# Block 1 attention: the reciprocal row sums are widened on GpSimd and turned by two more half transposes in the next unit's run, in place of two spreading matmuls

## What is computed

```python
s = jnp.einsum('bqhgd,bkhd->bhgqk', qi, k_all)
p = softmax_f32(s, v_all.dtype)
return jnp.einsum('bhgqk,bkhd->bqhgd', p, v_all)
```

## Time and profile before

| | |
|---|---|
| median of 3 runs | 2471.14 us |
| lowest, highest | 2470.4, 2471.89 us |
| profiled execution, its time | 2470.0 us |
| its span, first to last instruction | 2468.2 us |
| TensorE matmul, weight load | 2403.5, 1965.8 us busy |
| VectorE, ScalarE, GpSimd | 1337.6, 948.7, 470.7 us busy |
| mean granted TensorE clock | 0.992 |

### The profile page before, as it was taken

How to read it: one execution, slowest core, us unless ns; L and a number is a source line. 1 busy time by engine, 2 the same in 40 slices (tenths; PEclk the granted TensorE clock), 3 DMA queues, 4 the chain that set the end, 5 groups by cost and what they waited for, 6 DMA issues and landing times.

```text
span 2468.2 us, 39988 instructions
## 1 busy us (share of the span) xinstructions
PE 2403.5 (97%) x16150; PEld 1965.8 (80%) x16150; DVE 1337.6 (54%) x2653; ACT 948.7 (38%) x1659; POOL 470.7 (19%) x287
## 2 busy tenths in 40 slices
PE   8999999999999999999999999999999999999998
PEld 6778878888877788888887678888888667888887
DVE  5677667655236655667549444333336844433333
ACT  5473272632233724463453334222225323322222
POOL 2101211012342022103563231000014241000001
PEclk9999999999999999999999999999999999999999
DMA  8303413043233053306332112233232112223222
GB/s 316 113 2 124 167 50 120 22 159 140 64 116 137 2 205 112 117 35 239 105 139 81 52 60 88 90 96 104 89 99 96 60 52 69 94 77 120 94 79 75
DMA packets 64648, 250.49 MB, mean 101 GB/s; under 512 B 7888, under 2 KB 10448, under 8 KB 54992
## 3 DMA queue, kind: packets, MB, share of 16 engines
q1 hardware_dynamic: 61216, 236.10, 27.4%
q0 software_dynamic: 2592, 11.54, 1.4%
q10 hardware_dynamic: 656, 0.30, 0.1%
HBM read 243.67 MB, written 4.19 MB: 100 GB/s over the span
## 4 chain that ended last, share of the span: by engine, by line
PE 86%; ACT 4%; DVE 3%; issue 3%; POOL 2%; DMA 1%; ACTq 0%; SPq 0%; DVEq 0%; POOLq 0%
PE ps L2656 38%; PE ps L2467 21%; PE ps L593 5%; PE ps L692 4%; PE ps L2633 4%; PE ps L634 3%; ACT probs L866 2%; PE ps L677 2%; PE ps L2446 1%; PE ps L2349 1%; POOL split_panels_first L1121 1%; DMA stage_low<-in_ada 1%; PE ps L2673 1%; PE ps L2488 1%; PE ps L2601 1%
## 5 line engine op out<-in xcount | busy, mean ns | idle before, releaser
L2656 PE MATMUL ps<-h_split,split_panels 128*128 128x512 f32 x2928 | 685.6, 393 | 1.7 <-ACT projected L1580 0.7
L2656 PEld LDWEIGHTS ps<-h_split,split_panels 128*128 128x128 f32 x2928 | 545.9, 188 | 126.6 <-issue 13.6
L2467 PE MATMUL ps<-h_split_first,split_panels_first 128*128 128x512 f32 (+1 forms) x2772 | 543.6, 353 | 3.8 <-POOL h_split_first L1153 2.0
L2467 PEld LDWEIGHTS ps<-h_split_first,split_panels_first 128*128 128x128 f32 x2772 | 443.8, 189 | 78.1 <-issue 9.5
L1121 POOL TENSOR_TENSOR split_panels_first<-panels_first,split_panels_first 128x1024 fp32r<-128x1024 f32 (+1 forms) x102 | 229.0, 2246 | 711.7 <-ACT split_panels_first L1308 711.7
L1990 DVE TENSOR_TENSOR split_panels<-panels,split_panels 128x1024 fp32r<-128x1024 f32 (+2 forms) x171 | 192.6, 1126 | 297.0 <-ACT split_panels L1316 293.3
L1316 ACT ACTIVATE split_panels<-panels 128x1024 fp32r<-128x1024 f32 (+2 forms) x210 | 204.2, 974 | 344.9 <-PE ps L2656 343.5
L1814 DVE SCALAR_TENSOR_TENSOR ps<-modulation_panels,silu_c,ps 128x256 f32<-128x256 f32 x480 | 225.3, 488 | 29.7 <-issue 1.3
L2656 PE MATMUL ps<-ffn_hidden_split,split_panels 128*128 128x512 f32 x990 | 225.0, 389 | 0.0
L2656 PEld LDWEIGHTS ps<-ffn_hidden_split,split_panels 128*128 128x128 f32 x990 | 185.8, 188 | 38.6
L1132 POOL TENSOR_TENSOR probs_turned<-probs_turned,probs 128x512 f32<-128x512 f32 x30 | 42.3, 1411 | 771.3 <-ACT probs L1523 771.3
(11 more groups left out here) (304 smaller groups left out, 2975.2 us busy)
## 6 DMA issues: line engine op xcount, KB each, us to landing
modulation_panels<-in_ada SPq DMA_DIRECT2D x64, 1024.0 KB, 4.8
panels<-in_w SPq DMA_DIRECT2D x88, 512.0 KB, 3.3
panels_first<-in_in SPq DMA_DIRECT2D x72, 512.0 KB, 5.7
panels<-in_in SPq DMA_DIRECT2D x42, 512.0 KB, 3.3
panels_first<-in_out SPq DMA_DIRECT2D x32, 384.0 KB, 3.1
panels<-in_w SPq DMA_DIRECT2D x32, 384.0 KB, 3.1
panels<-in_w SPq DMA_DIRECT2D x32, 320.0 KB, 2.8
panels<-in_out SPq DMA_DIRECT2D x16, 512.0 KB, 3.3
```

The lines of the kernel that those rows point to most:

```text
L2467: ins = mm(at0, split1[:, s, w, c, :], hs1[:, h, c, lo:e], start=c == 0 and i == 0, stop=c == KC - 1 and i == 2)
L2656: ins = mm(out, split[:, n % SPLIT, a, c - base, :], moving(b, c), start=first and i == 0 and j == 0, stop=last and i == len(chunks) - 1 a ...
```

## The change

GpSimd gets one more task per unit. It multiplies ones by the column of reciprocals, repeated 64 times, for each head, and writes both into `wide_weights` (128x128). It waits for `weight_ready` and, since there is one buffer, until the run that read its last content has ended. TensorE's run for `prev` now starts with a half transpose of `wide_weights` partitions 0 to 63 of `old` into the output bank and ends with that of partitions 64 to 127; the pairs between are shifted by one. Before the run TensorE waits for the values, for `y_done`, for `weights_wide` and for `exp_done`, and before its last half for `low_weights`, which its own first half raises. `outputs_pe` makes no spreading matmuls for block 1. The last unit of a mixer gets a run of this one pair. Block 2 keeps its spreading.

```diff
-        def turn_halves_pe(pe, u):
-            pe.wait_ge(exp_done, 2 * u["u"] + 2)
+        def turn_halves_pe(pe, u, old):
             low, high, n_third = [], [], 0
+            if old:
+                pe.wait_ge(values_taken, old["values_seen"])
+                if old["i"] >= 1:
+                    pe.wait_ge(y_done, old["u"])
+                pe.wait_ge(weights_wide, old["u"] + 1)
+                low.append((bank(old["out_bank"], P, P + HD), wide_weights[0:HD, :]))
+            if u:
+                pe.wait_ge(exp_done, 2 * u["u"] + 2)
...
+            if old:
+                high.append((bank(old["out_bank"], P + HD, 2 * P), wide_weights[HD:P, :]))
             for n, two in enumerate(zip(low, high)):
...
+                for half, (to, src) in enumerate(two):
+                    if old and half == 1 and n == len(high) - 1:
+                        pe.wait_ge(low_weights, old["u"] + 1)
+                    ins.append(nc.tensor.transpose(to, src, ident[rows_of(half), HD * half:HD * half + HD]))
+                    if old and half == 0 and n == 0:
+                        ins[0].then_inc(low_weights, 1)
...
             pe.wait_ge(values_taken, u["values_seen"] + o.w)
-            spread_weights_pe(pe, u, o)
+            if not u["in_sets"]:
+                spread_weights_pe(pe, u, o)
...
-                if prev and not (m == "C" and i == 1):
-                    turn_probs_pe(pe, prev, o)
+                if (prev or old) and not (m == "C" and i == 1):
+                    turn_halves_pe(pe, prev, old)
...
         def attention_pool(pool, plan):
             for step in plan:
-                u = step["unit"]
+                u, prev = step["unit"], step["prev"]
                 if u and "band" in u:
                     pool.wait_ge(max_ready, 2 * u["u"] + 2)
...
+                if prev:
+                    s = 2 * prev["i"] % 4
+                    pool.wait_ge(weight_ready, prev["u"] + 1)
+                    if prev["u"] >= 1:
+                        pool.wait_ge(turned, prev["events"][-1]["t"] + 1)
+                    for e in range(2):
+                        ins = nc.gpsimd.tensor_tensor(wide_weights[:, HD * e:HD * e + HD], ones[:, 0:HD],
+                                                      weight[:, s + e:s + e + 1].to_broadcast([P, HD]), ALU.mult)
+                    ins.then_inc(weights_wide, 1)
```

More of the change, by code:

```diff
@@ L253, in two_dit_blocks @@
         weight = sb("row_weight", [P, 4])
+        wide_weights = sb("wide_weights", [P, P])
         y_weights = sb("weights_of_y", [P, P])
@@ L373, in two_dit_blocks @@
         turned, pt_by_act, pt_by_dve, values_taken = (sem(n) for n in ("turned", "pt_by_act", "pt_by_dve", "values_taken"))
-        pv_steps, y_done, half_filled, high_in_third = (sem(n) for n in ("pv_steps", "y_done", "half_filled", "high_in_third"))
+        pv_steps, y_done, half_filled, high_in_third, weights_wide, low_weights = (
+            sem(n) for n in ("pv_steps", "y_done", "half_filled", "high_in_third", "weights_wide", "low_weights"))
         u_ready = sem("u_ready")
@@ L613, in free_bank @@
                 pe.wait_ge(pt_by_dve, b["c"] + 1)
-        def turn_halves_pe(pe, u):
-            pe.wait_ge(exp_done, 2 * u["u"] + 2)
+        def turn_halves_pe(pe, u, old):
             low, high, n_third = [], [], 0
-            for ev in u["events"]:
-                for n, (_, col, e, _) in enumerate(places(ev)):
-                    if ev["second"]:
-                        n_third = n + 1
-                        low.append((bank(u["set"][2], HD * n, HD * n + HD), e, col))
-                        high.insert(n, (bank(u["set"][2], 256 + HD * n, 256 + HD * n + HD), e, col))
-                    else:
-                        low.append((bank(u["set"][0], HD * n, HD * n + HD), e, col))
-                        high.append((bank(u["set"][1], HD * n, HD * n + HD), e, col))
+            if old:
[6 more added lines that the diff above has]
+                pe.wait_ge(exp_done, 2 * u["u"] + 2)
+                for ev in u["events"]:
+                    for n, (_, col, e, _) in enumerate(places(ev)):
+                        src = [probs[rows_of(half), u["probs_at"], e, col:col + P] for half in range(2)]
+                        if ev["second"]:
+                            n_third = n + 1
+                            low.append((bank(u["set"][2], HD * n, HD * n + HD), src[0]))
+                            high.insert(n, (bank(u["set"][2], 256 + HD * n, 256 + HD * n + HD), src[1]))
+                        else:
+                            low.append((bank(u["set"][0], HD * n, HD * n + HD), src[0]))
+                            high.append((bank(u["set"][1], HD * n, HD * n + HD), src[1]))
+            if old:
+                high.append((bank(old["out_bank"], P + HD, 2 * P), wide_weights[HD:P, :]))
             for n, two in enumerate(zip(low, high)):
@@ L633, in turn_halves_pe @@
                     pe.wait_ge(high_in_third, u["z"])
-                ins = [nc.tensor.transpose(to, probs[rows_of(half), u["probs_at"], e, col:col + P], ident[rows_of(half), HD * half:HD * half + HD])
-                       for half, (to, e, col) in enumerate(two)]
-                if n == n_third - 1:
+                ins = []
+                for half, (to, src) in enumerate(two):
[4 more added lines that the diff above has]
+                        ins[0].then_inc(low_weights, 1)
+                if n_third and n == n_third - 1:
                     ins[1].then_inc(high_in_third, 1)
-            for half in range(2):
-                ins[half].then_inc(turned, 1)
+            if u:
+                for half in range(2):
+                    ins[half].then_inc(turned, 1)
         def turn_probs_pe(pe, u, o):
-            if u["in_sets"]:
-                turn_halves_pe(pe, u)
-                return
             pe.wait_ge(exp_done, 2 * u["u"] + 2 + o.u * 2)
@@ L713, in attention_pe @@
                 if m == "C" and i == 1:
-                    turn_probs_pe(pe, prev, o)
+                    turn_halves_pe(pe, prev, None)
                 if i == 1:
```

## The result

| | before | after |
|---|---|---|
| median of the runs compared | 2470.77 us (4 runs) | 2488.32 us (4 runs) |
| lowest, highest | 2469.33, 2471.89 | 2485.45, 2495.37 |
| profiled execution: time, span | 2470.0, 2468.2 | 2489.79, 2487.9 |

The ratio is 1.0075, 95% interval 1.0063 to 1.0088: 0.75% slower. The forecast was 2482.5 us with a range of 2473 to 2494, and 0.80 for slower. Direction and range held; the rise was 17.5 us where 11.7 was forecast (in the profiled executions 19.8 against 11.6).

What follows compares the result with a forecast made beforehand. TensorE, busy 97% of the span, was taken as the bound, with the last-ending path differing by stage. Stage terms summed to +11.6 us on 2470.0; with the median 1.1 above, 2482.7, said as 2482.5 (range 2473 to 2494).

Steps and rivals of the forecast that it cites:

- The start of B: First steps of B, both layers: the widening queues behind GpSimd's panel and band DMA, run 2.18 us late; +4.4 us.
- the fall of the clock there: Rival: TensorE's clock falls at B's start as idle time grows; 2 to 8 us more, 2485 to 2490; chance 0.06.
- B of layer 0: Groups of B, layer 0: band DMA delays and a y wait against five savings of 0.17 us; +2.5 us.
- plus 0.05 us to be seen by TensorE: GpSimd's price: after 0.58 us for both heads' widening, TensorE sees the result 0.05 us later.
- B of layer 1: B without context units: 15 savings of 0.17 us (-2.6) against band DMA delays (+1.4); -1.1 us.
- two loops are equally long here: Long units of A: ScalarE's loop and TensorE's two-unit path tie, so the longer run lengthens ScalarE's; +1.6 us.
- my sign that the run must grow by a tenth: Refutation test: the prediction is wrong if the run of transposes does not grow by a tenth; long runs +0.10 us.
- Context units: Context units of A and C: the run is on the loop, the spreading is not; 14 intervals of 0.16, +2.2 us.
- Tails and passages: Passages from long to context units, y wait, +0.9 us; lone-pair runs at the ends of six stages, +0.9 us.
- The equal case: Rival: widened weights are in time and only TensorE's stream balance counts; 2467 to 2476 us; chance 0.13.
- the whole-record case: Rival: a transpose takes its whole 227 ns record in TensorE's stream, not 66; +18 us, 2500 us; chance 0.02.
- The change pays: Rival: TensorE's stream ends last in more steps, winning 0.17 us in 60 to 80 units; 2458 to 2466; chance 0.07.

Runs made afterwards that it cites:

- e1: The changed kernel with GpSimd's first steps of B, up to the first widening, put ahead of the panel in its queue; 2481.01 us.
- e8: The kernel before, spreading kept, with TensorE's second run of each B waiting for a GpSimd widening queued behind the panel; 2476.87 us.
- e3: The changed kernel with B's first widening ahead of the panel and the band DMA behind the widening in GpSimd's queue; 2477.52 us.
- e5: The changed kernel, but GpSimd fills the wide weights once with a constant and TensorE never waits for it; 2476.37 us.
- e10: e3 with only the order of the four waits changed, so that the exponentials' wait stands on the weight load; 2474.54 us.
- e11: e3 with only the order of the four waits changed, so that the exponentials' wait stands two stops ahead of the load; 2480.26 us.
- e7: e3 with pair and waits half-way in the run, used only in the first 15 units of A (each layer) and B (layer 1); 2466.58 us.
- e12: e9 with the wait for y written ahead of that for the values, moving it from two stops to one; 2468.08 us.
- e9: The unit selection of e7, with the pair and its waits at the head of the run; 2469.78 us.

## Why the prediction was right in direction and short by a third

- **The start of B: the mechanism right, a rival came with it.** 2.18 us late were forecast and 2.23 measured. I had given the fall of the clock there 0.06 as a case of its own. It is no alternative to the wait, it follows from it: with 2.7 us of idle time it came behind five of six waits and cost 1.5 to 1.6 us, once 2.7 (against the same steps without a fall, e1 and layer 0 of e8). Its price here, 3.1 us for both layers, was in the range that I gave (2 to 8 us), its chance was not.
- **B of layer 0: mis-sized, 5.4 against 2.5 us.** The band DMAs were sized well: the forecast has 4.3 us for them (0.58 three times, 0.63 four times), and after less e3 is 3.8. The failed terms are the others, one y wait of 0.40 a group against five savings of 0.17: together -1.8 us in the forecast, +1.6 measured, in e3 and also in e5, where TensorE never waits for GpSimd. In both kernels TensorE waits for y in two steps of a group, the fourth unit's and the next, at 0.32 us each in the first three groups; I had counted one, though the y that ends at 354.33 is the one that the fourth unit's own run, at 353.98, would have to wait for the earlier trace rows. The savings were mostly 0.15, and none at the first unit of a group (+0.09). In the kernel after, the widening covers the y wait of the fourth unit (0.50 to 0.61 in place of 0.63). The first unit of a group cost 0.81 in place of 0.58: there the term "plus 0.05 us to be seen by TensorE" failed, which was 0.25, since this wait stands at two stops. At the two starts of B, where only three waits are written, it stands at one stop and was 0.09 (317.91 to 318.00). The Trainium skill (DMA: Bandwidth & Descriptors, Specifications and SWDGE vs HWDGE vs iDMA) had led to an estimate of +6 us, had GpSimd been busy with descriptors for 1 us. The trace disagrees with that use of the figure: the widening starts at 333.95, 0.60 us behind the issue at 333.35.
- **B of layer 1: +0.7 against -1.1.** Without the DMAs ahead (e3) it is -1.0, so they cost 1.7 us, near the forecast 1.4. The saving was 0.10 us a unit, not 0.17: the run of 9 pairs takes 0.71 us to the next instruction where that of 8 took 0.59, and what followed it, spreading and outputs, became shorter by 0.21 instead of 0.27.
- **A: wrong in sign, -1.1 against +1.6.** The step "two loops are equally long here" failed. I had taken a step in which ScalarE shows no idle time as a step that its loop bounds. Had it been so, a longer run would lengthen two steps from 8.67 us. e10 shortens them by 0.18 us, which is what the other path was forecast to save (0.17). So the path through TensorE and VectorE's minimum is the bound in both steps, and the kernel after loses half of its gain again to the later start of the run. The run itself grew by 0.03 us (0.92 to 0.95), not by 0.10; my sign that the run must grow by a tenth came true in B and the context units, and not here.
- **Context units: right, +2.6 against 2.2, with the parts mixed up.** Each was to grow by 0.16 and grew by 0.17. But 0.06 of it goes with the order of the waits alone (e10: +0.11 a unit; e11: +0.28), and only the rest is the pair and the wait on its first half (0.39 to 0.50 us from the run to the outputs or spreading).
- **C: mis-sized, +2.7 with the starts against +0.2.** The long units, +1.2 us, are at 0.0 in e10: the order of the waits again. In the start of C in layer 1 the clock fell, which is 1.0 us (+1.3 there in after, +0.3 in e3, where it did not fall).
- **Tails and passages: +0.8 against 1.8.** The lone pair takes somewhat more than was worked out. In the kernel after, TensorE:

```profile
199.39 0.60 PE L653 MATMUL ps<-matrices,wide_weights 64*128 64x64 f32 x2
199.92 0.33 PE L711 MATMUL ps<-probs,qkv 128*64 128x128 f32 x2
```

0.53 us from the pair to the outputs, where the forecast has 0.42 (0.27 and 0.15). The passages into the context units are in their stage above.
- **The rivals.** GpSimd did not answer late (294 ns), though TensorE heard of it late. The equal case and the whole-record case are refuted: runs of 13 pairs take 0.95 us in the stream (13 whole records of 227 ns would be near 3). On the Trainium skill's 275 ns a transpose (TensorE: Matmul & The Clock Gate, Part 4: PE-mode transpose) the trace disagrees as a price in the stream: the 13th pair of a run added 0.03 us, with records of 220 to 270 ns each. "The change pays" was held against by the wait for the exponentials in C and the context units, and that is just where it doesn't pay; where TensorE's path is the bound it does (e7).

By the stages of the profiled executions, of the 18.3 us the two starts of B are 7.4 with their falls of the clock (after to e1), the band DMAs ahead of the widening 5.5 (after to e3 in the rest of B), the fall in C of layer 1 is 1.0, and the place of the waits some 4.5 (e3 to e10, without the two falls in e10). The rest, the longer short runs and the wait for y less the gain in A and in B of layer 1, comes to about nothing.

That the time stayed within the range is partly luck: A came out 2.7 us better than forecast, and B of layer 0 and C were 2.9 and 2.5 us worse for reasons that the forecast did not have.

## What to carry to other kernels

Before an edit makes an engine wait for another one's queue, list what stands in that queue at this moment, and put the new step ahead of it; that was worth 11 us here (after to e3). Where an instruction has several waits, look at the compiled order and let the one that comes last stand on the instruction itself (in these kernels that was the one written first). Move work only in the units whose bound it relieves: the same edit wins in A and in B of layer 1, and loses in the context units.

## What the hardware showed that I had not expected

- The delay from the last awaited result to the first matmul depends on where the wait stands: 0.05 us on the weight load, 0.09 to 0.15 one semaphore instruction ahead of it, 0.25 to 0.26 two ahead. It was so with the exponentials (e10, e3, e11), with y (e12, e9) and with GpSimd's weights (317.91 to 318.00, 334.50 to 334.75).
- The clock falls after short stalls too, and not each time. In the start of C TensorE is idle for 1.36 us in the kernel before and in e7 and e9 alike. Window 1066 to 1069 us of e7 and of e9:

```profile
1066.00:1069.00 3.00, 3.00 (x27) 2.67 (x29) 1.15 (x6) 2.58 (x5) 0.00 (x0) 0.50 0.02 5
```

```profile
1066.00:1069.00 3.00, 2.68 (x46) 2.25 (x42) 1.77 (x8) 2.58 (x5) 0.00 (x0) 1.00 0.02 5
```

The same code up to here in C, and the same stall; one is at 0.50 and one at 1.00. It cost e7 1.3 us. In the start of C of layer 1 the clock fell in 7 of the 14 profiled executions of this case, in layer 0 in 2. What decides it stays open.
- Fewer busy microseconds on the busiest engine went with a longer span: TensorE -3.6, the span +19.7.
